# Splitting the expert value table by experts instead of by columns in a one-layer hybrid attention and expert-lookup kernel

## The reference, cut to what matters

```
def chunk(xc):                                  # 128 tokens
    qc = (xc @ w_query).reshape(C, 8, 2, 128)
    s = einsum('chpd,hpnd->chpn', qc, sub_keys)
    top_s, top_i = top_k(s, 16)
    cand_s = top_s[:, :, 0, :, None] + top_s[:, :, 1, None, :]
    cand_i = top_i[:, :, 0, :, None] * 128 + top_i[:, :, 1, None, :]
    best_s, best_pos = top_k(cand_s.reshape(C, 8, 256), 16)
    expert_idx = take_along_axis(cand_i, best_pos)
    g = softmax(best_s)
    act = gelu(einsum('chkd,cd->chk', expert_u[expert_idx], xc))
    return einsum('chk,chkd->cd', g * act, expert_v[expert_idx])
```

## Time and profile before

| what | us |
|---|---|
| median of three runs | 1737.0 |
| the profiled execution, its own time | 1737.77 |
| its span | 1735.9 |
| DVE busy | 1315.3 |
| PE busy | 1300.8 |
| POOL busy | 889.8 |
| ACT busy | 413.4 |

### The profile page before, as it was taken

The page is one execution under the profiler, slowest core; times in us unless marked ns, Lnnn a source line. Parts: engine busy times, 40 slices in busy tenths (PEclk is TensorE's granted clock), DMA queues, the critical chain, the costliest instruction groups (busy, mean ns, idle before and its releaser), DMA issues.

```text
span 1735.9 us, 15043 instructions
## 1 busy us (share of the span) xinstructions
PE 1300.8 (75%) x4980; PEld 888.0 (51%) x4980; DVE 1315.3 (76%) x2030; ACT 413.4 (24%) x859; POOL 889.8 (51%) x546
## 2 busy tenths in 40 slices
PE   9999999999984552365556555566597999999950
PEld 7888887778883441122223323333265555555530
DVE  5554655556799999988889999898769665666678
ACT  5333443643110101001034433432054000000000
POOL 1000010000386887888888888888622733334365
PEclk9999999999997776566676788876597999999985
DMA  7886557158799999999999999999965999999998
GB/s 237 220 208 191 173 152 223 59 185 297 267 416 417 421 389 385 382 420 421 414 384 392 393 418 400 391 421 420 394 207 159 403 409 411 409 409 409 409 402 349
DMA packets 150233, 584.24 MB, mean 337 GB/s; under 512 B 15586, under 2 KB 28596, under 8 KB 117268
## 3 DMA queue, kind: packets, MB, share of 16 engines
q0 software_dynamic: 74384, 438.08, 63.2%
q1 hardware_dynamic: 75460, 144.37, 25.2%
q10 hardware_dynamic: 320, 0.93, 0.1%
HBM read 580.95 MB, written 2.36 MB: 336 GB/s over the span
## 4 chain that ended last, share of the span: by engine, by line
POOL 31%; PE 26%; DMA 19%; DVE 16%; issue 7%; ACT 1%; DVEq 0%; ACTq 0%; POOLq 0%
DMA v_rows<-in_peer_expert_v,pick_row 16%; POOL big L676 13%; POOL v_rows L656 11%; POOL more_rows L676 7%; PE ps L1664 6%; PE ps L1666 6%; PE ps L1665 6%; DVE big L1564 4%; DVE more_rows L1522 4%; DVE big L1522 3%; DMA more_rows<-in_peer_expert_u,pick_row 2%; PE ps L2066 1%; PE ps L2090 1%; DVE big L1544 1%; DMA big<-in_peer_expert_u,pick_row 1%
## 5 line engine op out<-in xcount | busy, mean ns | idle before, releaser
L656 POOL DMA_INDIRECT v_rows<-in_peer_expert_v,pick_row x256 | 354.0, 1383 | 292.6 <-DVE big L1564 208.8
L2066 PE MATMUL ps<-v_rows,diag 128*128 128x512 f32 (+1 forms) x480 | 284.8, 749 | 210.4 <-DMA v_rows<-in_peer_expert_v,pick_row 206.1
L1522 DVE CUSTOM_DVE_ANT_0 big<-big 128x2048 f32<-128x2048 f32 x154 | 351.0, 2287 | 45.6 <-DMA big<-in_peer_expert_u,pick_row 45.3
L1564 DVE SCALAR_TENSOR_TENSOR big<-v_rows,pick_w,big 128x1280 f32<-128x1280 f32 x175 | 271.6, 1552 | 130.7 <-DMA v_rows<-in_peer_expert_v,pick_row 126.2
L676 POOL DMA_INDIRECT big<-in_peer_expert_u,pick_row x154 | 299.1, 1942 | 49.2 <-issue 47.2
L2066 PEld LDWEIGHTS ps<-v_rows,diag 128*128 128x128 f32 x480 | 119.3, 265 | 361.9 <-DMA v_rows<-in_peer_expert_v,pick_row 236.0
L1003 DVE TENSOR_TENSOR split_lo<-raw,split_hi 128x1024 fp32r<-128x1024 f32 x119 | 145.8, 1225 | 145.0 <-ACT split_hi L704 119.4
L1522 DVE CUSTOM_DVE_ANT_0 more_rows<-more_rows,big 128x2048 f32<-128x2048 f32 x102 | 232.1, 2286 | 21.5 <-DMA more_rows<-in_peer_expert_u,pick_row 21.1
L676 POOL DMA_INDIRECT more_rows<-in_peer_expert_u,pick_row x102 | 213.2, 2090 | 65.2 <-issue 28.0
L1664 PE MATMUL ps<-split_hi,ht 128*128 128x512 f32 x476 | 189.9, 399 | 1.2 <-DVE split_lo L1053 1.0
L2100 PE MATMUL ps<-big,dense 128*128 128x512 f32 (+1 forms) x512 | 187.5, 489 | 0.7 <-ACT big L931 0.7
(11 more groups left out here) (279 smaller groups left out, 1404.4 us busy)
## 6 DMA issues: line engine op xcount, KB each, us to landing
big<-in_peer_expert_v SPq DMA_DIRECT2D x128, 384.0 KB
raw<-in_w_in SPq DMA_DIRECT2D x88, 512.0 KB, 3.7
raw<-in_w_out SPq DMA_DIRECT2D x32, 512.0 KB, 5.3
big<-in_peer_w_query SPq DMA_DIRECT2D x16, 512.0 KB, 6.6
raw<-in_peer_w_query SPq DMA_DIRECT2D x8, 512.0 KB, 7.7
spare<-in_peer_w_query SPq DMA_DIRECT2D x8, 512.0 KB, 13.1
v_rows<-in_peer_expert_v,pick_row POOLq DMA_INDIRECT x256
big<-in_peer_expert_u,pick_row POOLq DMA_INDIRECT x154, 9.7
```

The costliest lines, as they stand in the source:

```text
L656: pool.indirect_dma_start(v_row(k), None, v_table, bass.IndirectOffsetOnAxis(pick_row[:, k:k + 1], 0)).then_inc(v_gathered[v_place(k)], 16)
L1522: dve.tensor_tensor_reduce(row, row, XN[:, place_of(m // TOPK)[0], :], 1.0, 0.0, ALU.mult, ALU.add, pick_dot[:, m:m + 1]).then_inc(dotted, 1)
L1564: dve.scalar_tensor_tensor(out=v, in0=row, scalar=pick_w[:, k:k + 1], in1=v, op0=ALU.mult, op1=ALU.add).then_inc(added, 1)
L2066: ins = pe.matmul(psf[:, c:c + w], diag[:, k % DIAGS, :], row[:, c:c + w], start=k == 0, stop=k == V_ON_PE - 1)
```

## The change

V is now split by experts. The experts whose first key is 86 or more (42 of 128 first keys, `DENSE_KEYS`, 5376 whole rows) are read in order, 42 loads of 128 rows of 8 KB, and multiplied with the matrix of weights. The others are gathered by pick as whole rows. A gather names all 128 rows as before, but carries a bound (`KEPT_ROWS` - 1 = 11007): indices above it are skipped. The place then keeps what it held in that partition, and the weight used for it, `pick_v`, is zero (`pick_w` times "first key below the bound"). `pick_v` shares the memory of `pick_act`.

V gathers now have eight places of 2048 elements (four in the U phase); PE adds the first 72 of them, and then every seventh from column 75 on (26 columns: 75, 82, ... 250), spread among the 42 dense loads; DVE adds the other 158. Both tiles' results accumulate in all eight PSUM banks. The weights' matrix has 42 first keys in place of 128; groups are of eight tokens, and a group's one-hot matrices are made by single wide instructions.

```
-V_ROW = 1280
-V_DENSE = D - V_ROW
+DENSE_KEYS = 42
+FIRST_DENSE = NKEYS - DENSE_KEYS
+KEPT_ROWS = FIRST_DENSE * NKEYS
-V_FIRST_PLACES, V_PLACES = 3, 6
-V_ON_PE = 80
+V_FIRST_PLACES, V_PLACES = 4, 8
+V_PE_EVERY, V_PE_FIRST = 7, 75
-GROUP_TOKENS = 4
+GROUP_TOKENS = 8
-HOT = 4
-TURN_0, GROUP_0, GROUP_EVERY, TURN_1 = 133, 140, 3, 246
+HOT = 2
+TURN_0, GROUP_0, GROUP_EVERY, TURN_1 = 133, 140, 6, 246

+def v_on_pe(k):
+    return k < V_BESIDE or (k - V_PE_FIRST) % V_PE_EVERY == 0
+LATE_PE = [k for k in range(V_BESIDE, PICKS) if v_on_pe(k)]
+def late_after(a):
+    return [k for j, k in enumerate(LATE_PE) if j and j * DENSE_KEYS // len(LATE_PE) == a]

 # SP
-            sp.wait_ge(dotted, PICKS)
-            for a in range(NKEYS):
+            sp.wait_ge(sem("scores"), HEADS)
+            sp.wait_ge(dotted, PICKS - RING)
+            for a in range(DENSE_KEYS):
                 if a == DENSE_EARLY:
-                    sp.wait_ge(token_made, TT * P)
+                    sp.wait_ge(dotted, PICKS)
                 if a >= DENSE_PLACES:
                     sp.wait_ge(dense_used, a - DENSE_PLACES + 1)
-                sp.dma_start(dense_rows[:, a % DENSE_PLACES, :], dense_src[:, a, V_ROW:D])
+                row = (FIRST_DENSE + a) * NKEYS
+                sp.dma_start(dense_rows[a % DENSE_PLACES], v_table[row:row + NKEYS, :])

 # POOL, v_gather(k)
-                if f < 0:
-                    pool.wait_ge(dotted, U_WIDE if v_place(k) < V_FIRST_PLACES else PICKS - len(NARROW) + 4)
-                elif f < V_ON_PE:
-                    pool.wait_ge(pe_added, f + 1)
+                if f < 0 and v_place(k) < 2:
+                    pool.wait_ge(dotted, U_WIDE)
+                elif f < 0 and v_place(k) < V_FIRST_PLACES:
+                    pool.wait_ge(query_used, QUERY_STEPS)
+                elif f < 0:
+                    pool.wait_ge(dotted, PICKS - len(NARROW) + v_place(k) - V_FIRST_PLACES + 1)
+                elif v_on_pe(f):
+                    pool.wait_ge(pe_added, pe_adds(f) + 1)
                 else:
-                    pool.wait_ge(added, f + 1 - V_ON_PE)
-                pool.indirect_dma_start(v_row(k), None, v_table,
-                                        bass.IndirectOffsetOnAxis(pick_row[:, k:k + 1], 0))
+                    pool.wait_ge(added, dve_adds(f) + 1)
+                pool.indirect_dma_start(v_rows[v_place(k)], None, v_table,
+                                        bass.IndirectOffsetOnAxis(pick_row[:, k:k + 1], 0),
+                                        bounds_check=KEPT_ROWS - 1, oob_is_err=False)

 # DVE, head_weights(n)
+                dve.wait_ge(sem("head_weighted"), 2 * n + 1)
+                dve.scalar_tensor_tensor(out=pick_v[:, v], in0=pick_keys[:, 0, v], scalar=float(KEPT_ROWS),
+                                         in1=pick_w[:, v], op0=ALU.is_lt, op1=ALU.mult)
 # DVE, the one-hot matrices
-                dve.tensor_scalar(hots[t][:, j % HOT, 0, :], iota[:, :], picks_t[:, 0, j:j + 1],
-                                  picks_t[:, 2, j:j + 1], ALU.is_equal, ALU.mult)
+                # hot_key: 8 tokens x 42 keys
+                dve.tensor_tensor(hot_keys[:, i % HOT, :, :], iota[:, FIRST_DENSE:NKEYS].unsqueeze(1).broadcast_to(hot_shape),
+                                  picks_of(0, i, DENSE_KEYS), ALU.is_equal)
+                # hot_weight: 8 x 42
+                dve.tensor_tensor(v, v, picks_of(2, i, DENSE_KEYS), ALU.mult)
+                # hot_half, tile 1: 8 x 128 (tile 0: by ACT, 8 squares and one relu)
+                dve.tensor_tensor(hot_halves[:, i % HOT, :, :], iota[:, :].unsqueeze(1).broadcast_to([P, GROUP_TOKENS, P]),
+                                  picks_of(1, i, P), ALU.is_equal)

 # DVE, after the last U dot
-            weigh(HEADS - 1)
-            dve.wait_ge(sem("picks_here"), 5)
-            for i in range(GROUPS):        # 32 groups of 4, with 8 v_adds
-            ...
-            for k in range(n, PICKS):
-                v_add(k)
+            hot_key(1, 0)
+            hot_half(0)
+            weigh(HEADS - 1)
+            hot_key(1, 1)
+            hot_half(1)
+            dve.wait_ge(sem("picks_here"), 5)
+            hot_weight(1, 0, GROUPS + 1)
+            hot_weight(1, 1, GROUPS + 2)
+            for i in range(HOT, GROUPS):
+                hot_key(1, i)
+                hot_half(i)
+                hot_weight(1, i, GROUPS + i + 1)
+            for k in range(PICKS):
+                if not v_on_pe(k):
+                    v_add(k)               # 2048 elements, to X[:, t, :]
+            for t in range(TT):
+                dve.wait_ge(sem("dense_end"), t + 1)
+                for h in range(2):         # X += PSUM, 1024 elements
+                    dve.tensor_tensor(X[:, t, v], X[:, t, v], psf[:, o:o + D // 2], ALU.add)

 # PE, after the last U dot
             for i in range(GROUPS):
                 group(1, i)
-                if i % 2 and V_BESIDE + i // 2 < V_ON_PE:
-                    pick_add(V_BESIDE + i // 2)
+                if i == GROUPS // 2:
+                    pick_add(LATE_PE[0])
-            for a in range(NKEYS):
+            for a in range(DENSE_KEYS):
                 dense(a)                   # 4 matmuls of 512 columns for each tile
+                for k in late_after(a):
+                    pick_add(k)            # 4 matmuls of 512 columns
```

More of the change, by code:

```diff
@@ L193, in v_at, with pe_adds, dve_adds @@
     return range(v_until(m - 1), v_until(m))
+def v_on_pe(k):
+    return k < V_BESIDE or (k - V_PE_FIRST) % V_PE_EVERY == 0
+def pe_adds(k):
+    return sum(v_on_pe(f) for f in range(k))
+def dve_adds(k):
+    return k - pe_adds(k)
+LATE_PE = [k for k in range(V_BESIDE, PICKS) if v_on_pe(k)]
 def group_at(m):
@@ L258, in layer @@
         pick_act = sb("pick_act", [P, PICKS])
+        pick_v = pick_act
         pick_w = sb("pick_w", [P, PICKS])
@@ L1553, in v_add @@
                 row = v_here(dve, k)
-                if k == PICKS - 1:
-                    dve.wait_ge(added, k - V_ON_PE)
-                    for h in range(2):
-                        v = slice(h * V_ROW // 2, (h + 1) * V_ROW // 2)
-                        dve.scalar_tensor_tensor(out=X[:, t, v], in0=row[:, v], scalar=pick_w[:, k:k + 1], in1=X[:, t, v],
-                                                 op0=ALU.mult, op1=ALU.add).then_inc(sem("half_added"), 1)
-                    return
-                if k > V_ON_PE:
-                    dve.wait_ge(added, k - V_ON_PE)
-                v = X[:, t, 0:V_ROW]
-                dve.scalar_tensor_tensor(out=v, in0=row, scalar=pick_w[:, k:k + 1], in1=v, op0=ALU.mult, op1=ALU.add).then_inc(added, 1)
-            def tile_out(n):
-                dve.wait_ge(pe_added, V_ON_PE)
-                if n:
-                    dve.wait_ge(added, n)
-                v = X[:, 0, 0:V_ROW]
-                dve.tensor_tensor(v, v, psf[:, 0:V_ROW], ALU.add).then_inc(sem("out_ready"), 1)
-                dve.wait_ge(sem("out_ready"), 1)
+                if dve_adds(k):
+                    dve.wait_ge(added, dve_adds(k))
+                dve.scalar_tensor_tensor(out=X[:, t, :], in0=row, scalar=pick_v[:, k:k + 1], in1=X[:, t, :],
+                                         op0=ALU.mult, op1=ALU.add).then_inc(added, 1)
             lo8, hi8 = slice(0, 8), slice(8, 16)
@@ L2062, in pick_add @@
                     pe.wait_ge(sem("pq_first"), 3)
[L2063 to L2066 removed]
+                pe.wait_ge(sem("diag_made"), j + 1)
+                for c in range(0, D, CHUNK):
+                    ins = pe.matmul(psf[:, t * D + c:t * D + c + CHUNK], diag[:, j % DIAGS, :], row[:, c:c + CHUNK],
+                                    start=k == 0, stop=False, skip_group_check=True)
                 ins.then_inc(pe_added, 1)
@@ new lines, in group @@
+                if g >= 2:
+                    pe.wait_ge(group_moved, g - 1)
+                pe.wait_ge(sem("hot_weighted"), g + 1)
+                if t:
+                    pe.wait_ge(sem("hot_half_dve"), i + 1)
+                else:
+                    pe.wait_ge(sem("hot_half"), (i + 1) * (GROUP_TOKENS + 1))
+                for j in range(GROUP_TOKENS):
+                    o = j * DENSE_KEYS
+                    ins = pe.matmul(ps[:, GROUP_BANK + i % 2, o:o + DENSE_KEYS], hot_halves[:, i % HOT, j, :], hot_keys[:, i % HOT, j, :],
+                                    start=True, stop=True)
@@ L2093, in dense @@
+                ins.then_inc(group_made, 1)
             def dense(a):
                 pe.wait_ge(dense_loaded[a % DENSE_PLACES], 16 * (a // DENSE_PLACES + 1))
-                row = dense_rows[:, a % DENSE_PLACES, :]
+                row = dense_rows[a % DENSE_PLACES]
                 for t in range(TT):
-                    for c, w in ((0, CHUNK), (CHUNK, V_DENSE - CHUNK)) if t == 0 else ((0, V_DENSE - CHUNK), (V_DENSE - CHUNK, CHUNK)):
-                        o = DENSE_BANK + t * V_DENSE + c
```

(12 more changed lines are left out.)

194 lines of the change are left out of this document (81 added, 113 removed).

## The result

The changed kernel takes 1795.4 us (median of four, 1789.3 to 1802.7) against 1737.9 for the kernel before in the same comparison: 1.0338 times as long, interval 1.0295 to 1.0382. It is slower by 3.4% where 0.35% faster was forecast, and outside the range of 1702 to 1772. Its profiled span is 1794.1 us.

What follows compares the result with a forecast made beforehand. DMA was taken to bound the U phase, DMA and PE most of the V phase; 1270 (last dot) + 40 (building) + 391 (V phase) + 4 (coupling) + 9 (end) + 16 (busiest engine) = 1730, median 1731, range 1702 to 1772.

Steps and rivals of the forecast that it cites:

- step 6: POOL's gathers in the V phase: 1.35 + 0.30 us each when nothing stops them, 2.1 available, so POOL hides.
- the coupling: V phase: DVE and PE wait for one another in one queue of places, 4 us, bounds 0 and 15.
- DMA's own need: V phase as DMA sees it: 1255 rows at 0.318 us, divided by 1.02, 391 us; the end adds 9.
- steps 1 to 3: U phase: V gathers beside it +7 us, tile 0's groups nothing, early dense loads +5; last dot at 1270.
- step 8: Whole kernel: skipped rows leave the busiest DMA engine more than the mean, 0 to 33 us, middle +16 taken.
- step 4: Building tile 1's weights: 40 us from last dot to DVE's first full-speed add, for 83; PE's upper bound 48.
- steps 5 to 7: After the building: V phase 391 us, coupling 4, POOL hidden, end 9 (PSUM adds and store).
- step 5: V phase: DMA 391 us, DVE 389, PE 376, three engines nearly even, plus 4 us of mutual waiting.
- rival "busiest engine": Both phases: the busiest DMA engine sets the pace, 37 + 105 rows too many, 45 us; 1760, chance 0.22.
- balanced: Rival: DMA engines stay even, or the busiest one's excess falls into idle time at the handover; 1715, chance 0.20.
- skipping isn't free: Rival, U and V phases: skipped rows take the time of read ones, U phase +67; 1910, chance 0.08.
- PE's clock: Rival, V phase: waits for gathers lower PE's clock to 0.87, so 376 us become 432; 1761, chance 0.10.

Runs made afterwards that it cites:

- e11: e3 with only half of each V row gathered, DVE and PE reading that half twice: 1745.5 us, one run.
- e4: Changed kernel with PE adding columns 72 to 79 between tile 1's groups, then every seventh from 82, DVE 151 columns: 1792.6 us, 1.0318.
- e3: Changed kernel with a fixed skip pattern, equally many skipped rows on every DMA engine, other V rows added than the reference's: 1761.2 us, 1.0133.
- e12: e3 with DVE adding only half of each row and PE leaving out tile 0's product for 40 of 42 dense blocks: 1737.5 us, one run.
- e10: e3 with DVE adding only the first 1024 of 2048 elements of each gather: 1740.7 us, one run.
- e16: e3 at full bytes with each DVE add of 2048 elements split into two of 1024: 1751.2 us, 1.0084.
- e9: e3 with six places for V gathers and not eight: 1780.9 us, one run.
- e6: Changed kernel with PE leaving out tile 0's product for 40 of 42 dense blocks, all loads kept: 1794.0 us, one run.
- e7: e3 with PE leaving out tile 0's product for 40 of 42 dense blocks: 1764.8 us, one run.
- e17: e4 with each DVE add split into two of 1024 elements, full computation: 1783.4 us, 1.0253.
- e1: Kernel before, its 5 KB V gathers given a bound no index passes, so nothing is skipped: 1737.9 us, 1.0017.

## Why the prediction was wrong, step by step

The sum was 1270 + 40 + 391 + 4 + 9 + 16 = 1730; the span is 1794.1. The mechanism that fits worst is step 6, which saw POOL as free; in size the terms that failed are the building (40, measured 57), the coupling (4, measured 24), DMA's own need (400 with the end, measured 416) and the busiest engine (16, measured 36).

- **U phase (steps 1 to 3): 1270, measured 1271.9.** Right as a number, by luck, as two errors cancel. With even skips it ends at 1261.9: instead of the priced +7 and +5 the phase grew by 4. The other 10 us are the busiest engine's, which the forecast had put in step 8. And that "DMA is the bound" left out that POOL was nearly full beside it: e11 took a priced 63 us from DMA there and won 8.
- **Building (step 4): 40, measured 57, a miss of 17.** The bound of 48 from above took 2.76 us for eight tokens from a row at full clock, where PE's adds stood between the groups. Nearly all of these went away with the change, and the short matmuls ran at half clock for most of it, 3.43 us a group (granted clock 0.56 from 1280 to 1300 us, 0.50 from 1320 on, and 1.00 only from 1314 to 1320, behind the one add). So PE held DVE back, whose own groups stood 1.98 us apart where nothing held them (priced 2.35). e4 shows it the other way round. The clock was listed as a rival, but for the V phase. DMA's lost time there is no smaller than before, 0.29 of 57 us against 0.57 of 83, 40 us against 36.
- **Rest (steps 5 to 7): 404, measured 465, a miss of 61.** Three parts. (a) Uneven engines: 26 us (e3). (b) DMA's own need: 416 and not 400 (e12). 3 us of the 16 are the pattern's 0.05 rows. 5 are the price of a row: e12 has 416 GB/s from 1400 to 1600 us, 0.316 us a row of an engine, where 0.318 / 1.02 = 0.312 was taken. 6 are the start: its first 20 us run at 299 GB/s. The last 2 were not separated. (c) 439 - 416 = 24 us, for which the step had "coupling, 4". 19 of them go when DVE has less to do (e10), 10 when its adds are only split (e16), although it then works longer: that much is the hold on POOL. What remains, some 14 us, was not resolved further; mutual waiting with eight places would fit (e9 says that places matter), but is not shown.
- **Step 6 (POOL hides) is the step that failed outright.** It read 1.35 + 0.30 us as POOL's free price. It was DVE's beat: its adds of 1280 stood 1.656 us apart in that stretch, the gathers 1.65. A free gather with the bound takes 0.99 + 0.30. What this step cost is, as far as e16 shows, 10 of the 61 us. With adds of 2048 the beat is 2.46, and 176 gathers at it would be 433 us, more than any term of step 5. The two rows stood side by side, and their equality was not seen.
- **Step 8 (busiest engine): 16 taken from 0 to 33; measured 36** (10 in the U phase, 26 after). Counted phase by phase by the dealing of the Trainium skill (DMA: Bandwidth & Descriptors, The descriptor swizzle), the estimate would have been 15 and 18 us. The count of whole phases prices too little in the V phase: the busiest engine has 46 rows more than each has in e3. With e12's 416 us they make 416 + 15, and the changed kernel takes 465, 35 us over this bound, where e3 is 24 over its own. Counted over the picks by the same dealing, the fullest engine has on average 7.6 rows of a single gather, where the mean engine has 5.45. That gathers wait for their own last engine, which e3 took away as well, would explain the other 11 us; no run separates it. The rival "busiest engine" (1760) named the mechanism and the side; its price was near, and what it lacked was the building and POOL.
- The rivals "balanced" and "skipping isn't free" are out (3370 packets of 4 bytes), and so is "PE's clock" for the V phase: the granted clock was 0.92, but PE's relief changed nothing (e6, e7).

The miss of 64 us adds up: 2 (dot) + 17 (building) + 61 (rest) - 16 (already counted).

## What to carry to other kernels

A gather that skips rows saves bytes, but each DMA engine keeps the rows of its partitions: price the busiest engine, by counting, not the mean, and take the count as the least that it costs. Before an instruction's duration is taken as its price, compare the distance between its records with the beat of the other engines in that stretch; if they are equal, it is a wait. And a clock read from a stage holds only for what the engine did in that stage: the 0.87 of the building before was 0.62 in the one after.

## What the runs showed that was not expected

- DVE adds of float32 with both inputs in SBUF, back to back, let one gather of POOL's through per instruction: 2.46 us apart beside adds of 2048, 1.65 beside adds of 1280. A held gather's busy time on the page is mostly waiting (2.15 us for 0.99). Two adds of 1024 for one of 2048 cost DVE 0.12 us more and took 10 and 9 us off (e16, e17).
- Groups of short matmuls of 42 columns ran at a granted clock of 0.50 to 0.56 though PE was busy 54 of 57 us; in e4, with an add of four 512-column products after every second group, it was 1.00 from 1295 to 1333 us, and eight adds fitted into the time of one.
- A skipped index costs a packet of 4 bytes, 9 ns; the bound itself costs POOL 0.05 us a gather and the kernel nothing that can be measured (e1, 1.0017).
